# Two units instead of one by token halves ahead of norms 1 to 3 of a decoder trunk

## The chip, the cores and the metric

One core of one Trainium2 chip runs the whole kernel. The metric is the device time of one execution in microseconds. The trace comes from one profiled execution, times in it are microseconds from its start.

## The reference, cut to what matters

The input x is 512 tokens by 1024 channels in float32. Each of two layers does

```python
h = _modulate(_rmsnorm(x, norm_mix_g[l]), shift1, scale1)
x = x + gate1[:, None, :] * _mixer(h, ...)          # ends with: merged @ w_mix_out
h2 = _modulate(_rmsnorm(x, norm_mlp_g[l]), shift2, scale2)
u = jnp.square(jax.nn.relu(h2 @ w_up[l]))
x = x + gate2[:, None, :] * (u @ w_down[l])
```

and `_rmsnorm(x, final_g)` closes the trunk. A norm needs the mean of x*x over all 1024 channels of a token, so it can't begin for a token before the last channels of x have been added. The norms are numbered 0 (layer 0, mixer), 1 (layer 0, MLP), 2 (layer 1, mixer), 3 (layer 1, MLP) and 4 (final).

## The kernel before, in words

**Layout.** x is held transposed, `x_T`: 8 tiles k of 128 channels, 512 tokens wide. Every matrix product of 32-bit values is three matmuls of a shorter format: weights and activations are split into a high half (`w_hi`, `h_hi` or `y_hi`) and the rest (`w_lo`, `h_lo` or `y_lo`), and the products hi*hi, hi*lo and lo*hi are summed in PSUM.

**Units.** The work of TensorE is cut into units of 256 output channels, with two halves j of 128 channels. `half_unit` (line 940) does one half for all 512 tokens: 8 tiles k by 3 matmuls, 24 in all, into the bank `proj[:, j]`. A unit's weights pass four hands. SyncE issues the load into `w_raw` (line 330; it waits until the low halves of the unit two before are made). ScalarE copies `w_raw` to `w_hi` (`split_weights`, line 464; in one operation, or in two pieces). GpSimd makes `w_lo` (line 425, four operations for each half of a unit, always in the order of the units). TensorE waits on `lo_ready`. `w_hi` and `w_lo` have four slots, that is two units: the weights of unit u + 2 can be split only when TensorE has ended the products of the same half of unit u, which ScalarE's `products` waits for.

**Ahead of a norm.** The last four units ahead of norms 1 to 3 (the mixer's output, units MIX to MIX+3, or the last quarter of the MLP's down projection, MLP+4 to MLP+7) each add two tiles of x. For a whole tile VectorE adds the product (`add_to_x`, line 1405), ScalarE squares the new x (`square`, line 447) and VectorE sums the squares (`add_square`, line 1300). The first three units go so. The last goes by token halves in `tail_unit` (line 1052): t is a half of 256 tokens, and the order is t=0 j=0, t=0 j=1, t=1 j=0, t=1 j=1, 24 matmuls of 256 columns each. Its adds are at lines 1413 (t=0) and 1416 (t=1), its squares at 452, its sum at 1308.

**The norm.** In the middle of the part t=1 j=0, TensorE does `mean_square` for t=0 (lines 1019 and 1021, a product with `ones`). ScalarE's `root` makes 1/sqrt by a logarithm and an exponential (495, 496). Then come 16 steps g, 8 tiles for t=0 and 8 for t=1. Each has a scale on VectorE into PSUM (`scale_step`, line 1425, on two alternating banks, so it waits for the low step two before), the high half on ScalarE (`high_half`, line 550) and the low half on VectorE (`low_step`, line 1432). Between them lie VectorE's remaining adds, and on ScalarE the root for t=1 (after g=4) and, at g = 6 to 9, the four pieces of the split of the unit after the next one.

**The normed unit.** The first unit behind the norm (`normed_unit`, line 1074, its matmuls at 1088) takes h as it comes: for t=0 tile by tile, j=0 and j=1 in turn, and for t=1 four tiles so and then the last four of j=0 and of j=1. Before the first matmul of each j it waits for that half's `lo_ready`. After the first two tiles of t=0 stands `mean_square` for t=1. TensorE takes its instructions strictly in this order, and so do the other engines.

## Time and profile before

| | us |
|---|---|
| runs shown | 2303.15, 2302.43, 2303.00; median 2303.0 |
| the profiled execution's own time | 2302.98 |
| its span, first to last instruction | 2301.3 |
| TensorE busy | 2273.9 (99% of the span) |
| VectorE busy | 1089.3 (47%) |
| ScalarE busy | 908.0 (39%) |
| GpSimd busy | 1147.4 (50%) |
| granted TensorE clock, mean | 0.999 |

A row of a timeline has the start, the duration, the engine, the line, the operation and its tiles (out<-in), the count where equal neighbours are merged, and in brackets how long the engine had been idle before it and which instruction released it. PE is TensorE, DVE VectorE, ACT ScalarE, POOL GpSimd, SPq the issuing queue of SyncE. Matmuls are pipelined: the time from the start of one to the start of the next says what one costs, not its duration.

### The profile page before, as it was taken

The page shows a single profiled execution, that of the slowest core. Times are in us where ns is not written, and L with a number is a line of the kernel's source. Part 1 is how long each engine was busy: PE and PEld are TensorE (multiplying, and loading weights), DVE is VectorE, ACT ScalarE, POOL GpSimd, SP SyncE. Part 2 cuts the span into 40 slices and gives each one's busy share as a digit, 9 for nine tenths or more (in the row PEclk, how much of TensorE's full clock was granted, in tenths as well). Part 3 has the DMA queues.
Part 4 walks back from the last instruction along what each step waited for, and adds up shares of the span by engine and source line. Part 5 has one row for each costly group of instructions (what it writes and reads, how often), then busy time and mean ns, then how long its engine had stood idle before and what let it go on. Part 6 is the DMA issues. An engine that isn't in the chain of part 4 may idle for free.

```text
span 2301.3 us, 28143 instructions
## 1 busy us (share of the span) xinstructions
PE 2273.9 (99%) x11378; PEld 1885.8 (82%) x11378; DVE 1089.3 (47%) x1497; ACT 908.0 (39%) x1125; POOL 1147.4 (50%) x1489
## 2 busy tenths in 40 slices
PE   7999999999999999999999999999999999999999
PEld 4888888888888888888888888888888788888887
DVE  5776568546653341121276757441666524221223
ACT  4332233256675242332333323232666834332332
POOL 3454554534455554555545455455444444555543
PEclk9999999999999999999999999999999999999999
DMA  9444544322222323323334444222222223233231
GB/s 300 135 151 147 169 133 146 129 74 74 74 92 74 107 86 101 101 92 93 109 120 151 160 141 139 78 92 92 76 72 73 74 92 92 96 103 95 92 97 69
DMA packets 244161, 252.49 MB, mean 110 GB/s; under 512 B 4016, under 2 KB 241728, under 8 KB 244032
## 3 DMA queue, kind: packets, MB, share of 16 engines
q1 hardware_dynamic: 242352, 247.00, 33.2%
q10 hardware_dynamic: 1680, 3.70, 0.5%
q8 instruction: 90, 1.47, 0.3%
q14 instruction: 39, 0.32, 0.0%
HBM read 248.59 MB, written 2.10 MB: 109 GB/s over the span
## 4 chain that ended last, share of the span: by engine, by line
PE 95%; DVE 2%; SPq 1%; DMA 1%; ACT 1%; issue 0%; DVEq 0%; ACTq 0%
PE proj L953 66%; PE proj L975 6%; PE proj L1009 4%; PE proj L992 4%; PE att L992 4%; PE att L1137 3%; PE att L1187 2%; PE att L1197 1%; PE att L1175 1%; PE att L1120 1%; PE proj L1070 1%; DVE att L1425 1%; SPq L339 1%; DVE h_lo L1432 1%; PE att L1150 1%; DMA first_y<-in_w_ada 1%
## 5 line engine op out<-in xcount | busy, mean ns | idle before, releaser
L425 POOL TENSOR_TENSOR w_lo<-w_raw,w_hi 128x256 fp32r<-128x256 f32 x1472 | 1145.3, 811 | 1124.3 <-ACT w_hi L471 985.5
L953 PE MATMUL proj<-h_hi,w_hi 128*128 128x512 f32 x1440 | 567.4, 394 | 0.0
L953 PE MATMUL proj<-h_hi,w_lo 128*128 128x512 f32 x1440 | 561.2, 390 | 0.0
L953 PE MATMUL proj<-h_lo,w_hi 128*128 128x512 f32 x1440 | 560.6, 389 | 0.0
L471 ACT ACTIVATE w_hi<-w_raw 128x1024 fp32r<-128x1024 f32 (+1 forms) x342 | 353.2, 1039 | 454.0 <-PE proj L953 278.5
L953 PEld LDWEIGHTS proj<-h_hi,w_lo 128*128 128x128 f32 x1440 | 270.3, 188 | 57.5
L953 PEld LDWEIGHTS proj<-h_hi,w_hi 128*128 128x128 f32 x1440 | 270.5, 188 | 56.3 <-issue 1.6
L953 PEld LDWEIGHTS proj<-h_lo,w_hi 128*128 128x128 f32 x1440 | 270.6, 188 | 54.1
L953 PE MATMUL proj<-y_hi,w_hi 128*128 128x512 f32 x800 | 311.2, 389 | 0.0
L953 PE MATMUL proj<-y_lo,w_hi 128*128 128x512 f32 x800 | 311.2, 389 | 0.0
L953 PE MATMUL proj<-y_hi,w_lo 128*128 128x512 f32 x800 | 311.2, 389 | 0.0
L1405 DVE SCALAR_TENSOR_TENSOR x_T<-proj,mod,x_T 128x512 f32<-128x512 f32 x72 | 54.1, 751 | 290.0 <-PE proj L953 290.0
L1318 DVE SCALAR_TENSOR_TENSOR slab<-slab,c_act 128x256 f32<-128x256 f32 x280 | 176.9, 632 | 9.9
L953 PEld LDWEIGHTS proj<-y_lo,w_hi 128*128 128x128 f32 x800 | 150.2, 188 | 31.3
L953 PEld LDWEIGHTS proj<-y_hi,w_lo 128*128 128x128 f32 x800 | 150.2, 188 | 31.2
L953 PEld LDWEIGHTS proj<-y_hi,w_hi 128*128 128x128 f32 x800 | 150.2, 188 | 31.0
L1713 DVE TENSOR_TENSOR work<-work 128x512 f32<-128x512 f32 x64 | 45.7, 714 | 207.0 <-ACT work L804 207.0
L480 ACT ACTIVATE w_hi<-w_raw 128x512 fp32r<-128x512 f32 x64 | 37.0, 625 | 200.8 <-PE proj L992 130.9
L804 ACT ACTIVATE work<-proj 128x512 f32<-128x512 f32 x64 | 38.2, 597 | 159.4 <-PE proj L953 156.9
L1614 DVE TENSOR_TENSOR_SCAN slab<-slab,work 128x1280 f32<-128x1280 f32 x32 | 91.4, 2855 | 1.1
L1612 DVE SCALAR_TENSOR_TENSOR work<-att,work 128x1280 f32<-128x1280 f32 x32 | 47.6, 1487 | 61.0 <-ACT work L702 61.0
L1009 PE MATMUL proj<-w_hi,h_hi 128*128 128x256 f32 x256 | 73.1, 286 | 0.0
(252 smaller groups left out, 3202.8 us busy)
## 6 DMA issues: line engine op xcount, KB each, us to landing
w_raw<-in_w_in SPq DMA_DIRECT2D x88, 1024.0 KB, 5.1
slab<-in_w_ada SPq DMA_DIRECT2D x42, 1024.0 KB, 6.7
w_raw<-in_w_up SPq DMA_DIRECT2D x32, 1024.0 KB, 5.3
w_raw<-in_w_down SPq DMA_DIRECT2D x32, 1024.0 KB, 5.1
w_raw<-in_w_ret_out SPq DMA_DIRECT2D x16, 1024.0 KB, 5.4
w_raw<-in_w_sb_out SPq DMA_DIRECT2D x8, 1024.0 KB, 5.1
w_raw<-in_w_mix_out SPq DMA_DIRECT2D x8, 1024.0 KB, 5.1
first_y<-in_w_ada SPq DMA_DIRECT2D x4, 1024.0 KB, 12.4
```

Source lines behind the costliest of these rows:

```text
L425: ins = pool.tensor_tensor(w_lo[:, slot, k:k + 2, :], w_raw[:, s, k:k + 2, P * j:P * (j + 1)], w_hi[:, slot, k:k + 2, :], ALU.subtract)
L471: ins = act.activation(w_hi[:, 2 * s + j, ks, :], w_raw[:, s, ks, P * j:P * (j + 1)], ACT.Copy)
L953: last = pe.matmul(proj[:, j, :], w[:, slot, k, :], a[:, k, :], start=k == 0 and n == 0, stop=k == KT - 1 and n == 2)
L975: last = pe.matmul(proj[:, j, :], w[:, slot, k, :], a[:, k, :], start=k == 0 and n == 0, stop=k == KT - 1 and n == 2)
L992: last = pe.matmul(v_of(t).rearrange("p (a n) -> p a n", a=4), a[:, k, t * P:(t + 1) * P], w[:, :, k, :], start=k == 0 and n == 0, stop=k ...
L1009: last = pe.matmul(proj[:, t // 2, UNIT * (t % 2):UNIT * (t % 2 + 1)].rearrange("p (a n) -> p a n", a=2), a[:, k, t * P:(t + 1) * P], w[:, ...
L1137: last = pe.matmul(att[:, RET_BANKS[t], :], p[:, at:at + P], v[:, j, :], start=j == 0 and n == 0, stop=j == t and n == 2)
L1187: last = pe.transpose(att_flat[:, at:at + P], logits[:, a, row_at(i) + P * j:row_at(i) + P * (j + 1)], ident[:, :])
L1318: ins = dve.scalar_tensor_tensor(acc, raw[:, k, :], c_act[:, k:k + 1], acc, ALU.mult, ALU.add)
L1405: free(dve.scalar_tensor_tensor(x_T[:, k, :], proj[:, half, :], mod[:, ds(gate_col + k, 1)], x_T[:, k, :], ALU.mult, ALU.add), half)
L1612: own.link(dve.scalar_tensor_tensor(terms[:, a, :], scores_of(a), 0.0, terms[:, a, :], ALU.max, ALU.add))
L1614: own.link(dve.tensor_tensor_scan(logits[:, a, ::-1], carry_t[:, ::-1], terms[:, a, ::-1], 0.0, ALU.mult, ALU.add))
```

## The change

The last two units ahead of norms 1 to 3 go by token halves, together: `tail_units` does t=0 for both units (four parts of 24 matmuls of 256 columns), then t=1 for both. The first mean square stands in the middle of the first part of t=1. The second unit of the two writes to the two late banks in both halves; a semaphore `late_free` says that its t=0 values have been taken. Squares and sums of tiles 4 to 7 become operations of 256 columns each. On ScalarE the split of the normed unit's own weights (unit + 2) stands at g = 1 to 4 in pieces, and that of the unit behind it (unit + 3) at g = 9 to 12. The root for t=1 stands after the eight high halves of t=0. VectorE does its remaining adds and sums between the steps for t=0, and the last add behind the eighth low step. Counters of squares and sums are rebased (`SQUARED`, `SUMMED`). The tail ahead of the final norm keeps its order.

```diff
@@ -74,6 +74,9 @@
 HALVES = (slice(0, HALF), slice(HALF, SEQ))
 NORM_STEPS = 2 * KT
 BIG = 3.0e38
+
+SQUARED = (0, 10, 22, 34, 46)
+SUMMED = (0, 8, 18, 28, 38)
 
 RET_UNITS = 6
...
+            def square_part(n, k, t, buffers):
+
+                added_before = 3 * t + k - 2 if k >= 6 else k - 2
+                act.wait_ge(sq_used, SUMMED[n] + 1 + added_before)
+                act.activation(buffers[0][:, k % 2, HALVES[t]], x_T[:, k, HALVES[t]], ACT.Square).then_inc(squared, 1)
+
             def norm_tail(n, pair, unit, buffers):
 
-                tail_first(n, pair, unit, buffers)
-                for g in range(NORM_STEPS):
+                for j in range(2):
+                    added(pair, unit, j)
+                    square_part(n, 4 + j, 0, buffers)
+                for j in range(2):
+                    act.wait_ge(late_free, 2 * (n - 1) + j + 1)
+                    square_part(n, 6 + j, 0, buffers)
+                root(n, 0)
+                added(pair, unit + 1, 0)
+                square_part(n, 4, 1, buffers)
+                for g in range(KT):
                     high_half(n, g)
-                    if g == 3:
-                        tail_second(n, buffers)
-                    if g == 4:
-                        root(n, 1)
-                    if g in (6, 8):
-                        products(pair, unit, (g - 6) // 2)
-                    if 6 <= g < 10:
-                        split_weights(pair, unit + 2, (g - 6) // 2, g % 2)
+                    if g == 2:
+                        added(pair, unit + 1, 1)
+                        square_part(n, 5, 1, buffers)
+                    if g == 6:
+                        act.wait_ge(tail_added, 2 * n - 1)
+                        square_part(n, 6, 1, buffers)
+                    if g in (1, 3):
+                        products(pair, unit, g // 2)
+                    if g in (1, 2, 3, 4):
+                        split_weights(pair, unit + 2, (g - 1) // 2, (g - 1) % 2)
+                act.wait_ge(tail_added, 2 * n)
+                square_part(n, 7, 1, buffers)
+                root(n, 1)
+                for g in range(KT, NORM_STEPS):
+                    high_half(n, g)
+                    if g in (9, 11):
+                        products(pair, unit + 1, (g - 9) // 2)
+                    if 9 <= g < 13:
+                        split_weights(pair, unit + 3, (g - 9) // 2, (g - 9) % 2)
...
+            def tail_units(n, pair, unit, hi, lo, buffers):
+
+                for t in range(2):
+                    for m in range(2):
+                        for j in range(2):
+                            slot = 2 * ((unit + m) % 2) + j
+                            if t == 0:
+                                pe.wait_ge(lo_ready, 8 * pair + 4 * (unit + m) + 2 * (j + 1) + LO_CREDIT)
+                            if m == 0:
+                                pe.wait_ge(bank_free[j], 2 * pair + unit + 1 + t)
+                            elif t == 1:
+                                pe.wait_ge(late_free, 2 * (n - 1) + j + 1)
+                            dst = proj[:, j, HALVES[0]] if m == 0 else tail_late(j)
+                            for k in range(KT):
+                                if (t, m, j, k) == (1, 0, 0, KT // 2):
+                                    mean_square(n, 0, buffers)
+                                for i, (w, a) in enumerate(((w_hi, hi), (w_hi, lo), (w_lo, hi))):
+                                    last = pe.matmul(dst, w[:, slot, k, :], a[:, k, HALVES[t]],
+                                                     start=k == 0 and i == 0, stop=k == KT - 1 and i == 2)
+                            last.then_inc(tail_done if t == 0 else proj_done, 1)
...
-            def norm(n, between):
-
+            def add_part_square(n, k, t, buffers):
+
+                dve.wait_ge(squared, SQUARED[n] + 4 * t + k + 1)
+                dve.wait_ge(sq_used, SUMMED[n] + 3 * t + k)
+                sq_sum = buffers[1][:, HALVES[t]]
+                dve.tensor_tensor(sq_sum, sq_sum, buffers[0][:, k % 2, HALVES[t]], ALU.add).then_inc(sq_used, 1)
+
+            def add_part(n, k, t, pair, unit, gate_col):
+
+                m, j = (k - 4) // 2, k % 2
+                gate, x = mod[:, ds(gate_col + k, 1)], x_T[:, k, HALVES[t]]
+                if t == 0:
+                    dve.wait_ge(tail_done, 4 * (n - 1) + k - 3)
+                else:
+                    products(pair, unit + m, j)
+                ins = dve.scalar_tensor_tensor(x, proj[:, j, HALVES[0]] if m == 0 else tail_late(j), gate, x,
+                                               ALU.mult, ALU.add)
+                ins.then_inc(bank_free[j] if m == 0 else tail_added if t else late_free, 1)
+
+            def norm_tail(n, pair, unit, gate_col, buffers):
+
+                def part_of(k, t):
+                    add_part(n, k, t, pair, unit, gate_col)
+
+                add_square(n, 3, buffers)
+                part_of(4, 0)
+                part_of(5, 0)
+                add_part_square(n, 4, 0, buffers)
+                part_of(6, 0)
+                add_part_square(n, 5, 0, buffers)
+                part_of(7, 0)
+                add_part_square(n, 6, 0, buffers)
                 dve.wait_ge(mods_ready, n)
-                for g in range(NORM_STEPS + 1):
+                for g in range(KT):
+                    scale_step(n, g)
+                    if g == 0:
+                        part_of(4, 1)
+                    if g == 2:
+                        add_part_square(n, 4, 1, buffers)
+                    if g == 3:
+                        part_of(5, 1)
+                    if g >= 1:
+                        low_step(n, g - 1)
+                    if g == 4:
+                        add_part_square(n, 5, 1, buffers)
+                    if g == 6:
+                        part_of(6, 1)
+                    if g == 7:
+                        add_part_square(n, 6, 1, buffers)
+                low_step(n, KT - 1)
+                part_of(7, 1)
+                for g in range(KT, NORM_STEPS + 1):
                     if g < NORM_STEPS:
                         scale_step(n, g)
-                    if g in between:
-                        between[g]()
-                    if g >= 1:
+                    if g > KT:
                         low_step(n, g - 1)
-
-            def norm_tail(n, pair, unit, gate_col, buffers):
-
-                add_square(n, 5, buffers)
-                add_tail(n, 0, 0, pair, unit, gate_col)
-                add_last_square(n, 0, buffers)
-                add_tail(n, 1, 0, pair, unit, gate_col)
-                between = {0: lambda: add_tail(n, 0, 1, pair, unit, gate_col),
-                           2: lambda: add_last_square(n, 1, buffers),
-                           3: lambda: add_tail(n, 1, 1, pair, unit, gate_col)}
-                norm(n, between)
```

The loops ahead of the tails are one unit shorter on all engines: `range(2)` for `range(3)` ahead of norms 1 and 3, and two units for three in the last `down` of layer 0, with `norm_tail` and `tail_units` called on MIX + 2 and MLP + 6.

## Rows read from the trace of the kernel before

**Rows 1.** Timeline of TensorE around norm 1: start us, us, engine, line, operation.

```profile
785.79 0.39 PE L953 MATMUL proj<-h_hi,w_hi 128*128 128x512 f32 x1
...
796.67 0.28 PE L1070 MATMUL proj<-h_hi,w_hi 128*128 128x256 f32 x1
...
803.87 0.60 PE L1019 MATMUL att<-work,ones 128*128 128x256 f32 x2
...
804.85 0.28 PE L1070 MATMUL att<-h_lo,w_hi 128*128 128x256 f32 x1
...
809.04 0.28 PE L1088 MATMUL proj<-h_hi,w_hi 128*128 128x256 f32 x1
...
810.49 0.60 PE L1019 MATMUL att<-work,ones 128*128 128x256 f32 x2
...
822.49 0.39 PE L1088 MATMUL proj<-h_hi,w_hi 128*128 128x256 f32 x1
...
824.38 0.40 PE L953 MATMUL proj<-h_hi,w_hi 128*128 128x512 f32 x1
```

**Rows 2.** Waits of TensorE, whole run: us in total, times, longest us.

```profile
PE att L843 <- DMA decay_t<-in_final_g: 7.8, 1, 7.8
...
PE proj L1088 <- DVE h_lo L1432: 1.8, 6, 0.3
```

**Rows 3.** Timeline of VectorE around norm 1.

```profile
799.75 0.48 DVE L1413 SCALAR_TENSOR_TENSOR x_T<-proj,mod,x_T 128x256 f32<-128x256 f32 x1 [0.40 <-PE proj L1070]
...
800.72 0.90 DVE L1308 TENSOR_TENSOR work<-work 128x256 f32<-128x256 f32 x1 [0.49 <-ACT work L452]
...
805.88 0.49 DVE L1425 SCALAR_TENSOR_TENSOR att<-x_T,n_scale,att 128x256 f32<-128x256 f32 x1 [2.77 <-ACT att L496]
...
807.75 0.48 DVE L1432 SCALAR_TENSOR_TENSOR h_lo<-att,n_shift,h_hi 128x256 fp32r<-128x256 f32 x1 [0.51 <-ACT h_hi L550]
...
808.27 0.49 DVE L1425 SCALAR_TENSOR_TENSOR att<-x_T,n_scale,att 128x256 f32<-128x256 f32 x1
...
808.67 0.42 DVE L1308 TENSOR_TENSOR work<-work 128x256 f32<-128x256 f32 x1
...
814.54 0.49 DVE L1425 SCALAR_TENSOR_TENSOR att<-x_T,n_scale,att 128x256 f32<-128x256 f32 x1
...
821.95 0.48 DVE L1432 SCALAR_TENSOR_TENSOR h_lo<-att,n_shift,h_hi 128x256 fp32r<-128x256 f32 x1 [0.15 <-ACT h_hi L550]
```

**Rows 4.** Timeline of VectorE around norm 2.

```profile
1153.88 0.48 DVE L1413 SCALAR_TENSOR_TENSOR x_T<-proj,mod,x_T 128x256 f32<-128x256 f32 x1 [0.40 <-PE proj L1070]
...
1176.03 0.48 DVE L1432 SCALAR_TENSOR_TENSOR h_lo<-att,n_shift,h_hi 128x256 fp32r<-128x256 f32 x1 [0.15 <-ACT h_hi L550]
```

**Rows 5.** Timeline of ScalarE around norm 1.

```profile
800.26 0.42 ACT L452 ACTIVATE work<-x_T 128x256 f32<-128x256 f32 x1 [1.77 <-DVE x_T L1413]
...
806.88 0.42 ACT L452 ACTIVATE work<-x_T 128x256 f32<-128x256 f32 x1 [1.10 <-DVE x_T L1416]
...
807.24 0.84 ACT L550 ACTIVATE h_hi<-att,n_shift 128x256 fp32r<-128x256 f32 x2
...
814.46 0.62 ACT L471 ACTIVATE w_hi<-w_raw 128x512 fp32r<-128x512 f32 x1
...
832.40 1.04 ACT L471 ACTIVATE w_hi<-w_raw 128x1024 fp32r<-128x1024 f32 x1
```

**Rows 6.** Timeline of GpSimd around norm 1, operations merged (xcount).

```profile
798.05 3.28 POOL L425 TENSOR_TENSOR w_lo<-w_raw,w_hi 128x256 fp32r<-128x256 f32 x4 [2.17 <-ACT w_hi L471]
...
815.16 5.60 POOL L425 TENSOR_TENSOR w_lo<-w_raw,w_hi 128x256 fp32r<-128x256 f32 x8 [13.82 <-ACT w_hi L471]
```

**Rows 7.** Line 425 from 797.9 to 801.5 us: duration ns min/median/max.

```profile
L425 POOL TENSOR_TENSOR w_lo<-w_raw,w_hi x4: 737/741/1192, 798.1 to 800.6; 128x256 fp32r<-128x256 f32 x4
```

**Rows 8.** DMA issues of the page: KB each, us to landing.

```profile
w_raw<-in_w_up SPq DMA_DIRECT2D x32, 1024.0 KB, 5.3
```

**Rows 9.** First 20 us: busy us by engine, granted clock, DMA share, GB/s.

```profile
0.00:20.00 20.00, 8.16 (x50) 6.20 (x50) 7.62 (x17) 9.53 (x15) 2.10 (x17) 1.00 0.94 313
```

More of the change, by code:

```diff
@@ L788, in _ @@
                         split_weights(first, SB_OUT + m + 2, half)
-                for m in range(3):
+                for m in range(2):
                     for half in range(2):
@@ L794, in _ @@
                         square(2 * layer + 1, 2 * m + half, at_mlp)
-                norm_tail(2 * layer + 1, first, MIX + 3, at_mlp)
+                norm_tail(2 * layer + 1, first, MIX + 2, at_mlp)
                 if layer < DEPTH - 1:
@@ L810, in down @@
                 def down(pair, last):
-                    for m in range(3 if last else 4):
+                    for m in range(4 if not last else 2 if layer < DEPTH - 1 else 3):
                         for half in range(2):
                             products(pair, MLP + 4 + m, half)
-                            if not last or m < 2 or layer < DEPTH - 1:
+                            if not last or m < 2:
                                 split_weights(pair, MLP + 4 + m + 2, half)
@@ L1050, in turn_first_tokens, with final_unit @@
                             last.then_inc(y_turned, 1)
-            def tail_unit(n, pair, unit, hi, lo, buffers, final=False):
+            def final_unit(pair, unit, hi, lo, buffers):
                 for t in range(2):
                     for j in range(2):
-                        if final and t == j == 1:
+                        if t == j == 1:
                             turn_first_tokens(pair, unit)
@@ L1064, in tail_unit @@
                             if (t, j, k) == (1, 0, KT // 2):
[L1065 to L1068 removed]
+                                final_mean_square(0, buffers)
                             for m, (w, a) in enumerate(((w_hi, hi), (w_hi, lo), (w_lo, hi))):
@@ L1234, in _ @@
                 whole_unit(first, GB_LAST, h_hi, h_lo)
-                for m in range(7):
+                for m in range(6):
                     hi, lo, unit = (y_hi, y_lo, SB_OUT + m) if m < 4 else (h_hi, h_lo, SB_OUT + m)
@@ L1240, in _ @@
                         half_unit(first, unit, half, hi, lo, tile_ready if half == 0 else None)
-                tail_unit(2 * layer + 1, first, MIX + 3, h_hi, h_lo, at_mlp)
+                tail_units(2 * layer + 1, first, MIX + 2, h_hi, h_lo, at_mlp)
                 def quarter(pair, f):
@@ L1248, in quarter @@
                             whole_unit(pair, MLP + m, h_hi, h_lo)
-                    for m in range(4 if f < QUARTERS - 1 else 3):
+                    for m in range(4 if f < QUARTERS - 1 else 2 if layer < DEPTH - 1 else 3):
                         for half in range(2):
@@ L1257, in _ @@
                 quarter(first + 4 * (QUARTERS - 1), QUARTERS - 1)
-                tail_unit(2 * layer + 2, first + 4 * (QUARTERS - 1), MLP + 7, y_hi, y_lo, at_layer,
-                          layer == DEPTH - 1)
+                if layer < DEPTH - 1:
+                    tail_units(2 * layer + 2, first + 4 * (QUARTERS - 1), MLP + 6, y_hi, y_lo, at_layer)
+                else:
+                    final_unit(first + 4 * (QUARTERS - 1), MLP + 7, y_hi, y_lo, at_layer)
             n = 2 * DEPTH
@@ L1295, in add_square @@
                 if 1 <= k <= KT - 2:
-                    dve.wait_ge(squared, 10 * n + (k + 1 if k < 6 else 8))
+                    dve.wait_ge(squared, SQUARED[n] + (k + 1 if k < 6 else 8))
                     if k >= 2:
-                        dve.wait_ge(sq_used, 8 * n + k)
+                        dve.wait_ge(sq_used, SUMMED[n] + k)
                     sq, sq_sum = buffers[0], buffers[1]
@@ L1687, in _ @@
                 gates = MODS * KT * layer
-                for m in range(7):
+                for m in range(6):
                     for half in range(2):
@@ L1702, in _ @@
                             add_to_x(first, SB_OUT + m, half, k, gates + KT * GATE1)
-                norm_tail(2 * layer + 1, first, MIX + 3, gates + KT * GATE1, at_mlp)
+                norm_tail(2 * layer + 1, first, MIX + 2, gates + KT * GATE1, at_mlp)
                 def quarter(pair, f, last):
@@ L1717, in quarter @@
                                               ALU.subtract).then_inc(u_split, 1)
-                    for m in range(3 if last else 4):
+                    for m in range(4 if not last else 2 if layer < DEPTH - 1 else 3):
                         for half in range(2):
```

30 lines of the change are left out of this document (14 added, 16 removed).

## The prediction, made before the changed kernel ran

> **What bounds the kernel now.** I read the page first (TensorE busy in 99% of the span), then TensorE's waits, then the timelines around one norm, engine by engine. TensorE is the bound nearly everywhere, so only two things about a norm can move the time: how much TensorE is given to do there, and where it is held up. All times t below count from the start of the last unit but one ahead of norm 1, at 785.79 us [rows 1].
>
> The reader is to see four marks on TensorE [rows 1]: the last unit begins at t=10.88 (48 matmuls of 512 columns behind, 0.227 us each); the normed unit begins at 23.25; its mean square comes 1.45 us into it; and the next unit begins at 38.59. A matmul of 256 columns costs 0.120 us from start to start (35 of them between 804.85 and 809.04), and a mean square in the middle adds 0.86 us (803.87 to 804.85 less one matmul). The 192 matmuls of 256 columns between t=10.88 and 38.59 are worth 23.0 us, the two mean squares 1.8. So 27.71 - 24.8 = 2.9 us are lost in small gaps before matmuls of the normed unit. The list of waits names only 1.8 us for all norms together, six waits of 0.3 us at most [rows 2]; the rest is too short to be listed but is there in the sum.
>
> These gaps come from VectorE's chain. The scale of step 8 starts at t=28.75 and the low half of step 15 at 36.16 [rows 3]: 7.41 us for eight steps, 0.91 to 0.93 each, while TensorE needs 0.72 for a tile (six matmuls). The last low half sets the end: the tile's first matmul starts 0.54 us behind it (822.49), then 15 matmuls remain, and 824.38 is reached. The second norm has the same distance from its first late add to its last low half, 22.15 us against 22.20 [rows 3, 4], and the six waits are two for each of three norms. I take the three as equal, and their losses as 8.7 us together: the most that the change could give back.
>
> **The change, part by part.** *Matmuls.* One more unit goes in 96 matmuls of 256 columns in place of 48 of 512: 11.50 us for 10.88, so +0.62 us for each norm, on TensorE itself, with nothing to hide it. The normed unit can start at t=23.87 at the earliest.
>
> *The first root.* The mean square for t=0 now stands at 4.5 parts, t=12.94. Its sum waits for the add of tile 7, t=0, which can start at 11.71: the part ends at 11.50, and the first late add started 0.20 us behind its part (796.67 plus 24 matmuls is 799.55; 799.75 in [rows 3]). Its square starts 0.51 us later [rows 3, 5] and ends at 12.64, in time. From the mean square to the first scale took 2.01 us [rows 1, 3]. So the first scale is at 14.95 where it was at 20.09, and the first eight steps have nine microseconds ahead of the normed unit. The gaps of its first half go.
>
> *The order on VectorE and ScalarE.* I follow it with these lags, all from rows: 0.49 from a dependent scale or add to the next on VectorE, 0.40 if independent (808.27 to 808.67), 0.51 to ScalarE's operation on it, 0.36 from a square to the next operation, 0.51 from a high half to its low half, 0.52 from that to the next scale on its bank [rows 3, 5]. Scale 0 at 14.95, add of tile 4 (t=1) 15.44, its square 15.95, high half 0 16.31, low half 0 16.8, scale 2 17.3, low half 1 18.1, scale 3 18.6, add of tile 5 19.0, its square 19.5. Only then comes the second piece of the split of the normed unit's weights, half j=0, at 19.87; the pieces for j=1 follow behind high halves 3 and 4, the last at 21.7. Before, these weights had been split in whole operations during the last plain unit, and their low halves were made by 801.33 (t=15.5) [rows 6]; nobody waited.
>
> *The low halves.* A piece takes 0.62 us and GpSimd starts 0.08 behind its end (814.46 and 815.16) [rows 5, 6]. So GpSimd starts on half j=0 at 20.56. Four operations take 2.80 us when nothing disturbs them (5.60 for eight) and 3.28 when one is stretched from 0.74 to 1.19 us [rows 6, 7]. Half j=0 is ready at 23.4 to 23.8, just as TensorE comes to it. Half j=1 is ready at 26.2 to 27.1, and TensorE needs it at 24.2, behind the first three matmuls. It stands for 2.0 to 2.9 us. This wait is new. Behind it on TensorE are all further matmuls, and among them the mean square for t=1, so ScalarE's root, VectorE's scale 8 and everything of the second half wait for it as well.
>
> *The second half.* After the wait come nine matmuls (1.08 us) and the mean square at 27.3 to 28.2. The add of tile 7 (t=1), late in VectorE's list, is at 25.5 to 26.3 and its square by 27.2, so that cover holds. Then +2.01 to scale 8 at 29.4 to 30.3, against 28.75 before, +7.2 to 7.4 to the last low half (the pieces of the next unit's split stand between its high halves, as four did in the first half before), +0.54 and 1.80 for 15 matmuls: the end is at 38.9 to 39.9, where it was 38.59. TensorE has kept pace by then: from the mean square, 0.86 and 87 matmuls give 38.6 to 39.5, less than the chain by 0.3.
>
> *Which value.* The low halves decide. VectorE's sum of squares with both inputs in SBUF (line 1308) took 0.90 us beside GpSimd and 0.42 alone [rows 3], and one of GpSimd's four operations was stretched by 0.45 in the stretch where two such sums (one of 512, one of 256 columns) ran [rows 6, 7]. The new order puts two 256-column sums, of tiles 5 and 6, into the 5.7 us of GpSimd's work. Between no stretch and a full one for each, I take half: +0.4 on the lower end, the nearest row being one in which a smaller sum cost VectorE rather than GpSimd. With 0.1 for the split pieces in the chain, the end is at about 39.3 to 39.4: +0.7 us a norm.
>
> The Trainium skill (SBUF — State Buffer, section "Who interferes with whom") says that a VectorE instruction with two SBUF inputs and a GpSimd instruction that reads SBUF lock each other out, the later one standing until the first ends. By that rule both sides pay at each meeting, and the sum would go to its upper end, +1.2 us a norm. The two durations of line 1308 agree with it.
>
> *What else moves, at nothing.* The 256-column adds, squares and sums of tiles 4 and 5 replace whole ones and lie beside TensorE's parts with 1 us or more to spare; if that cover went, the mean square for t=0 would be late by the excess. The loads: the unit behind the normed one had its low halves by t=35.0 [rows 6], now by 38.2 to 40, so SyncE issues the load two units on about 4 us later. It lands 5.3 us on [rows 8], at 43.5 to 45.3, and ScalarE splits it at 46.6 [rows 5] plus the shift of the end. The cover left is about 2 us. In norm 2 the loads behind it on SyncE's queue (the ada rows) move with it.
>
> **The sum.** 3 x (+0.7) = +2.1 us. The profiled execution took 2302.98, the median is 2303.0, so the sum stands against either: 2305. The bounds are 3 x 0.3 and 3 x 1.3: 2303.9 to 2306.9. About 0.2% (4.6 us) is what a measurement of this kernel can tell from no change.
>
> **The rivals.** *A: the split comes early enough.* If TensorE hardly waits for j=1 (the pieces earlier, or GpSimd faster than in any row), the add of tile 7 and its square set the mean square at about 26.1, scale 8 comes at 28.1 and the end at 37.6: -1.0 us a norm, 2300. If VectorE's chain kept pace too, only TensorE's own 0.62 and one mean square would be left: 36.3, -2.3 a norm, 2296, the only way to a measurable gain. For it: 9 us of room for the first eight steps. Against it: the square of tile 5 stands ahead of the split on ScalarE, and 2 x 2.8 us of GpSimd's work can't fit into the 3.6 us from 20.56 to 24.2.
>
> *B: the pause costs TensorE its clock.* The place is the new wait at the second half of the weights, 2 to 3 us in one piece, where today no wait around a norm is over 0.3. If the granted clock fell there from 2.4 to 1.2 GHz for the rest of the normed unit, its 93 matmuls would take 0.12 us more each: +11 us for a norm, and slower than 2303 by over 4.6 from a single such norm: 2316 for one, 2338 for three. Against it: in the first 20 us of the run TensorE is busy for 8.2 us only, with a first wait of 7.8 us, and its granted clock is 1.00 [rows 2, 9]. The Trainium skill (TensorE: Matmul & The Clock Gate, "Why this matters for your kernels") warns that idle gaps between bursts of matmuls bring the clock back to half; the trace here shows gaps as long without a fall.
>
> *C: GpSimd or the loads slip further.* If every one of the eight low operations were as stretched as the worst (1.19 us), they would end 3 us later than the upper end, +4 us a norm, 2315. It takes more than the two sums in 5.7 us; one stretched operation in four is all that rows show.
>
> **How the numbers follow.** The forecast (the wait for the low halves, +0.3 to +1.3 a norm) has 0.80. A without a measurable gain has 0.08, with one 0.03. B has 0.04, C and a load that lands too late 0.05. Faster by over 0.2%: 0.03. Within: 0.88. Slower: 0.09. The range is the forecast's 2303.9 to 2306.9, with 2 us below for lags that I have too long, towards A, and 0.6 above for a short slip of a load: 2301.8 to 2307.5.
>
> **What would show it.** In the changed profile: 0.62 us more of TensorE's matmuls a norm; the first scale 14.95 us behind the first tail unit's start; TensorE's longest wait at line 1088's successor, for GpSimd's line 425, three times, 2.0 to 2.9 us; scale 8 at 29.4 to 30.3; the normed unit's end at 38.9 to 39.9. No such wait, or a wait for ScalarE's square in its place, would be rival A; a granted clock under 1.00 in the normed unit, rival B; low operations of more than 3.3 us for four, rival C. The forecast falls if the time is under 2301 or over 2308.

## The result, and the profile after

| kernel | runs | lowest | median | highest (us) |
|---|---|---|---|---|
| before | 20 | 2302.43 | 2303.33 | 2304.33 |
| changed | 20 | 2304.79 | 2306.53 | 2308.37 |

One run of the kernel before took 3187.36 us, 880 us more than any other, and is left out of the highest value. The ratio is 1.0014 (95% interval 1.0008 to 1.002): the changed kernel is 3.2 us slower, within 0.2% and within the range. Its runs lie further apart, 3.6 us from lowest to highest against 1.9. The profiled execution took 2307.48 us.

The page's first lines, of the changed kernel:

```profile
span 2305.7 us, 28461 instructions
...
PE 2275.1 (99%) x11522; PEld 1894.5 (82%) x11522; DVE 1092.9 (47%) x1509; ACT 909.9 (39%) x1137; POOL 1145.3 (50%) x1489
```

TensorE is busy for 1.2 us more than before, the span is 4.4 us longer. The other 3.2 us are time in which TensorE stood. A stretch at a slower clock counts as busy. Of TensorE's waits (engine, line, releaser: us in total, times, longest), the second is new and answers to [rows 2]:

```profile
PE att L871 <- DMA decay_t<-in_final_g: 7.5, 1, 7.5
...
PE proj L1134 <- POOL w_lo L428: 6.2, 3, 2.1
```

Three waits for GpSimd's low halves, 6.2 us together, 2.1 at most, in place of six of 0.3 us for VectorE. The clearest look at them is norm 3, where the clock stays up. TensorE from the start of the two tail units (answers to [rows 1]):

```profile
1917.91 0.28 PE L1068 MATMUL proj<-h_hi,w_hi 128*128 128x256 f32 x1
...
1941.80 0.28 PE L1134 MATMUL proj<-h_hi,w_hi 128*128 128x256 f32 x1
...
1944.38 0.39 PE L1134 MATMUL proj<-h_hi,w_hi 128*128 128x256 f32 x1 [2.06 <-POOL w_lo L428]
...
1957.08 0.40 PE L981 MATMUL proj<-h_hi,w_hi 128*128 128x512 f32 x1
```

GpSimd there, eight low operations of the normed unit's weights:

```profile
1938.40 5.93 POOL L428 TENSOR_TENSOR w_lo<-w_raw,w_hi 128x256 fp32r<-128x256 f32 x8 [15.82 <-ACT w_hi L474]
```

VectorE there (the sums of squares of tiles 5 and 6 at line 1488, scale 8 at 1947.51, the last low half):

```profile
1939.11 0.99 DVE L1488 TENSOR_TENSOR work<-work 128x256 f32<-128x256 f32 x1
...
1942.90 0.85 DVE L1488 TENSOR_TENSOR work<-work 128x256 f32<-128x256 f32 x1
...
1947.51 0.88 DVE L1473 SCALAR_TENSOR_TENSOR att<-x_T,n_scale,att 128x256 f32<-128x256 f32 x2 [2.98 <-ACT att L499]
...
1954.65 0.48 DVE L1480 SCALAR_TENSOR_TENSOR h_lo<-att,n_shift,h_hi 128x256 fp32r<-128x256 f32 x1 [0.15 <-ACT h_hi L553]
```

Counted from 1917.91: the normed unit starts at 23.89, GpSimd starts at 20.49 and ends at 26.42, TensorE goes on at 26.5, scale 8 is at 29.60, the last low half at 36.74, the end at 39.17. In the kernel before the end was at 38.59, 38.81 and 38.53 around norms 1, 2 and 3. The two sums of squares beside GpSimd took 0.99 and 0.85 us where one alone takes 0.42 [rows 3].

Norm 1 of the same trace looks the same up to the wait, and then differs. TensorE by windows (window, length, busy us, granted clock, DMA share, GB/s):

```profile
808.00:812.00 4.00, 3.33 (x28) 1.00 0.01 4
...
812.00:814.00 2.00, 0.61 (x4) 0.94 0.00 0
...
814.00:817.00 3.00, 3.00 (x12) 0.50 0.77 224
...
817.00:820.00 3.00, 3.00 (x26) 0.97 0.35 125
...
1167.00:1170.00 3.00, 0.93 (x8) 1.00 0.01 3
...
1170.00:1173.00 3.00, 3.00 (x24) 1.00 0.78 246
```

The reader is to see three things: in the two windows from 808 to 814 TensorE stands idle for over 2 us; from 814 to 817 its granted clock is 0.50, that is 1.2 GHz; and in norm 2 (1167 to 1173) the same pause is followed by a clock of 1.00. In the slow stretch the matmuls of 256 columns come 0.21 to 0.22 us apart instead of 0.12:

```profile
810.81 0.28 PE L1134 MATMUL proj<-h_hi,w_hi 128*128 128x256 f32 x1
...
814.53 0.41 PE L1134 MATMUL proj<-h_hi,w_hi 128*128 128x256 f32 x1
...
814.75 0.41 PE L1134 MATMUL proj<-h_lo,w_hi 128*128 128x256 f32 x1
...
827.57 0.40 PE L981 MATMUL proj<-h_hi,w_hi 128*128 128x512 f32 x1
```

The normed unit of norm 1 takes 16.76 us (810.81 to 827.57), that of norm 3 15.27 (1941.81 to 1957.08). A fall of the clock costs 1.5 us here. Against the kernel before, the end comes 2.07 us later around norm 1 (40.66), and 0.64 later around norm 2 (39.45) and norm 3 (39.17). The stretches from one norm's end to the next tail's start are the same in both traces within 0.02 us.

There is one more, in a stage that the change doesn't touch. From 20 to 27 us, changed and before:

```profile
20.00:27.00 7.00, 6.34 (x28) 0.76 1.10 348
```

```profile
20.00:27.00 7.00, 4.77 (x28) 1.00 1.10 348
```

The same 28 matmuls, at a mean clock of 0.76 and of 1.00. The first tail unit starts at 786.91 instead of 785.79, 1.1 us later in this execution. So the 4.5 us between the two profiled executions are 1.9 for the normed units' later ends (3 x 0.64), 1.4 more for the fall at norm 1 and 1.1 ahead of all norms, in code that the change leaves as it was. That all of this 1.1 is the early fall's is not shown. In the five traces without an early fall the first tail unit (the last unit but one) starts at 785.79 to 786.39; in those with one it starts at 786.91, 787.03 and 787.09 (changed, e6, e1), but also at 785.96 and 786.15 (e7, e4), where the fall cost nothing visible.

### The profile page after: what moved, and what is told of

Same layout as the page of the kernel before. It is cut to its first block, busy times and chain, and to the rows that moved or that the text cites. A ratio compares the mean times of both kernels' runs of the same rounds, so it can differ in the third digit from the quotient of the medians.

```text
span 2305.7 us, 28461 instructions
## 1 busy us (share of the span) xinstructions
PE 2275.1 (99%) x11522; PEld 1894.5 (82%) x11522; DVE 1092.9 (47%) x1509; ACT 909.9 (39%) x1137; POOL 1145.3 (50%) x1489
## 4 chain that ended last, share of the span: by engine, by line
PE 95%; DVE 2%; ACT 1%; POOL 1%; issue 1%; DMA 0%; DVEq 0%; SPq 0%; ACTq 0%
PE proj L981 65%; PE proj L1003 6%; PE proj L1037 4%; PE proj L1020 4%; PE att L1020 4%; PE att L1183 3%; PE att L1233 2%; PE att L1243 1%; PE att L1221 1%; PE att L1166 1%; PE proj L1068 1%; PE proj L1134 1%; POOL w_lo L428 1%; PE att L1068 1%; PE att L1196 1%
## 5 line engine op out<-in xcount | busy, mean ns | idle before, releaser
L981 PE MATMUL proj<-h_hi,w_hi 128*128 128x512 f32 x1408 | 554.9, 394 | 0.0
L981 PE MATMUL proj<-h_hi,w_lo 128*128 128x512 f32 x1408 | 548.7, 390 | 0.0
L981 PE MATMUL proj<-h_lo,w_hi 128*128 128x512 f32 x1408 | 548.1, 389 | 0.0
L981 PEld LDWEIGHTS proj<-h_hi,w_lo 128*128 128x128 f32 x1408 | 264.2, 188 | 56.2
L981 PEld LDWEIGHTS proj<-h_hi,w_hi 128*128 128x128 f32 x1408 | 264.4, 188 | 55.4 <-issue 1.6
L981 PEld LDWEIGHTS proj<-h_lo,w_hi 128*128 128x128 f32 x1408 | 264.6, 188 | 52.5
L981 PE MATMUL proj<-y_hi,w_hi 128*128 128x512 f32 x784 | 305.0, 389 | 0.0
L981 PE MATMUL proj<-y_lo,w_hi 128*128 128x512 f32 x784 | 305.0, 389 | 0.0
L981 PE MATMUL proj<-y_hi,w_lo 128*128 128x512 f32 x784 | 305.0, 389 | 0.0
L981 PEld LDWEIGHTS proj<-y_lo,w_hi 128*128 128x128 f32 x784 | 147.1, 188 | 30.3
```

Source lines behind the costliest of these rows:

```text
L981: last = pe.matmul(proj[:, j, :], w[:, slot, k, :], a[:, k, :], start=k == 0 and n == 0, stop=k == KT - 1 and n == 2)
```

## The experiments

Two theories stand, and add: **the wait theory** (the low halves of the normed unit's weights hold TensorE, +0.6 us a norm) and **the clock theory** (the pause that this makes throws TensorE's clock in some executions, 1.5 us each time, and this spreads the runs and makes the rest of the difference). The rival to both: the extra narrow matmuls and something unseen.

All were timed in five rounds with the kernel before on the same chip, 11 runs each, e5 5 runs. The intervals of e1 and e6 include 1: by the runs alone these two can't be told from the kernel before.

| kernel | lowest | median | highest | ratio to before (95%) |
|---|---|---|---|---|
| e1 split early | 2301.29 | 2301.54 | 2302.30 | 0.9993 (0.9984 to 1.0001) |
| e2 pause filled | 2304.83 | 2305.73 | 2306.53 | 1.001 (1.0001 to 1.0019) |
| e3 narrow only | 2304.59 | 2305.06 | 2306.06 | 1.0009 (1.0 to 1.0018) |
| e4 order tuned | 2297.70 | 2298.12 | 2299.23 | 0.9978 (0.9969 to 0.9987) |
| before beside e1 to e4 | 2302.70 | 2303.22 | 2304.53 | |
| e5 split late | 2310.64 | 2312.47 | 2312.67 | 1.0039 (1.0025 to 1.0052) |
| r1 changed again | 2304.97 | 2306.23 | 2308.62 | 1.0012 (1.0004 to 1.0021) |
| before beside e5 and r1 | 2302.56 | 2303.17 | 2303.87 | |
| e6 vector order only | 2303.13 | 2303.72 | 2304.79 | 1.0003 (0.9994 to 1.0012) |
| e7 order tuned again | 2297.57 | 2297.93 | 2298.76 | 0.9978 (0.9969 to 0.9987) |
| before beside e6 and e7 | 2302.51 | 2303.10 | 2304.37 | |

### The narrow matmuls alone

```diff
@@ half_unit, of before.py @@
-                for k in range(KT):
+                for cols in HALVES if narrow else (slice(0, SEQ),):
+                    for k in range(KT):
...
-                        last = pe.matmul(proj[:, j, :], w[:, slot, k, :], a[:, k, :],
+                            last = pe.matmul(proj[:, j, cols], w[:, slot, k, :], a[:, k, cols],
```

`narrow` is set for the last unit but one ahead of norms 1 to 3.

> The kernel before, with the last unit but one ahead of norms 1 to 3 in matmuls of 256 columns by token halves, its order on all other engines as before. Theory: this term alone, 0.62 us a norm, 1.9 us: 2305.2 with before at 2303.3, no wait of TensorE over 0.3 us. Rival (the narrow matmuls are hidden in gaps of VectorE's chain): the chain starts later by the same time, so nothing hides; if they were hidden, 2303.3.

Measured 2305.06, 1.84 us over before beside it, where 1.86 (3 x 0.62) was worked out. The waits at the normed unit stay what they were:

```profile
PE proj L1089 <- DVE h_lo L1434: 1.8, 6, 0.3
```

So the price of the first part of the change stands whole on TensorE's path. The lowest run, 2304.59, is also within 0.2 us of the changed kernel's lowest, 2304.79, and in the traces the unit behind norm 3 ends at 39.19 here and at 39.17 in the changed kernel: what the earlier root gave back, the wait for the low halves took.

### The split of the weights earlier

```diff
@@ ScalarE's norm_tail, of the changed kernel @@
                 root(n, 0)
+                products(pair, unit, 0)
+                split_weights(pair, unit + 2, 0)
                 added(pair, unit + 1, 0)
...
-                    if g in (1, 3):
-                        products(pair, unit, g // 2)
-                    if g in (1, 2, 3, 4):
-                        split_weights(pair, unit + 2, (g - 1) // 2, (g - 1) % 2)
+                    if g == 1:
+                        products(pair, unit, 1)
+                        split_weights(pair, unit + 2, 1)
```

> Only ScalarE's split of the normed unit's weights is moved: half j=0 whole right behind the first root, half j=1 whole behind high half 1. Wait theory (the low halves hold TensorE): GpSimd starts 3.9 us earlier, the wait for it at the second half of the weights is gone, but a wait of 1.5 us in front of the second mean square takes its place, because the split delays the steps and the square of tile 7 by 0.5 us; the normed unit ends 38.3 us behind the first tail unit's start, against 38.6 before and 39.2 in the changed kernel without a clock fall: 2302.2. Clock theory (a pause of 2.3 us in one piece throws the clock now and then): with 1.5 us at most the falls around the norms get rare and the runs stand as close together as those of before. Rival (the extra matmuls and something else, not the weights, hold the time): no change against the changed kernel, 2304.8 or more.

2301.54, 1.7 us under before and 5.0 under the changed kernel, where 2302.2 was expected: only ScalarE's copies moved. GpSimd starts 3.8 us earlier, at 16.6 behind the start of the tail units (787.09):

```profile
803.73 5.99 POOL L428 TENSOR_TENSOR w_lo<-w_raw,w_hi 128x256 fp32r<-128x256 f32 x8 [11.97 <-ACT w_hi L474]
```

and TensorE takes the normed unit's first twelve matmuls without a wait, then stands at the second mean square:

```profile
787.09 0.28 PE L1069 MATMUL proj<-h_hi,w_hi 128*128 128x256 f32 x1
...
810.98 0.28 PE L1135 MATMUL proj<-h_hi,w_hi 128*128 128x256 f32 x1
...
812.42 0.65 PE L1048 MATMUL att<-work,ones 128*128 128x256 f32 x2
...
813.61 0.70 PE L1050 MATMUL att<-work,ones 128*128 128x256 f32 x2 [0.54 <-ACT work L574]
...
824.81 0.40 PE L982 MATMUL proj<-h_hi,w_hi 128*128 128x512 f32 x1
```

The mean square's second matmul starts 1.19 us behind its first, where 0.43 is usual; ScalarE's square of tile 7 (line 574) releases it. The wait there is 0.8 us, half of the 1.5 expected. The unit ends at 37.72 behind the start, 0.6 earlier than expected and 0.9 earlier than before; the three norms together make 2.5 us, but the medians show 1.7. The profiled execution of e1 has the fall in the window from 20 to 27 us and starts its first tail unit 1.3 us later than before. From norm 3's normed unit to the end of its span it takes 349.3 us where before (1952.60 to 2301.3) and the changed kernel (1957.08 to 2305.7) take 348.7; the 0.6 us lie behind the last matmul. How many of its other executions have either is not known, so 0.8 us stay open. The rival (nothing gained against the changed kernel) is out. Its runs span 1.0 us, the changed kernel's 3.6: without the long pause the spread goes, as the clock theory has it.

### The split of the weights later

```diff
@@ ScalarE's norm_tail, of the changed kernel @@
-                    if g in (1, 3):
-                        products(pair, unit, g // 2)
-                    if g in (1, 2, 3, 4):
-                        split_weights(pair, unit + 2, (g - 1) // 2, (g - 1) % 2)
+                    if g in (3, 5):
+                        products(pair, unit, (g - 2) // 2)
+                    if g in (3, 4, 5, 6):
+                        split_weights(pair, unit + 2, (g - 3) // 2, (g - 3) % 2)
```

> The changed kernel with the four pieces of the split two steps later (g = 3 to 6 instead of 1 to 4). Wait theory: GpSimd starts 1.3 us later, TensorE waits 1.0 us for half j=0 and 2.7 us for half j=1 of the normed unit's weights, and the unit ends 1.3 us later in each norm than in the changed kernel without a clock fall: its fastest runs are at 2304.8 + 3.9 = 2308.7. Clock theory: the pauses are longer (3.7 us with 0.4 us of work between them), so falls get more frequent, up to one in each norm at about 1.5 us: the median lies 2 to 5 us above the fastest runs. Rival (the weights are not what holds TensorE): no change against the changed kernel.

2312.47, and the lowest of five 2310.64, where the fastest were expected at 2308.7. Both weights' halves are waited for now, six times (us in total, times, longest):

```profile
PE proj L1134 <- POOL w_lo L428: 8.5, 6, 2.3
```

The profiled execution is the lowest one, and the clock fell in two of its three normed units (norms 1, 2 and 3 in turn):

```profile
813.00:816.00 3.00, 2.47 (x10) 0.50 0.38 84
...
1171.00:1174.00 3.00, 3.00 (x14) 0.57 0.76 241
...
1948.00:1951.00 3.00, 3.00 (x24) 1.00 0.71 204
```

Norm 3 has no fall and shows what the later split costs by itself:

```profile
1920.04 0.28 PE L1068 MATMUL proj<-h_hi,w_hi 128*128 128x256 f32 x1
...
1960.24 0.40 PE L981 MATMUL proj<-h_hi,w_hi 128*128 128x512 f32 x1
```

The end is at 40.20, 1.0 us later than in the changed kernel (39.17), where 1.3 was expected: 3.1 us for three norms. The two falls cost 1.3 and 1.2 us here (normed units of 16.93 and 17.05 us against 15.60 at norm 3, and 0.3 more at norm 2 in any kernel). 2310.64 less both is 2308.1, and the changed kernel's lowest run and 3.1 make 2307.9: the two agree. So the wait theory holds, a later split is a later end. That falls get more frequent rests on less: all five runs lie 2.7 us or more above 2307.9, which would be two falls or more in each. The longest single pause, 2.3 us, is hardly longer than the changed kernel's 2.1; another of 0.55 us stands ahead of it, with three matmuls between them.

### The pause filled

```diff
@@ normed_unit, of the changed kernel @@
+                            if t == k0 == 0 and j == 1:
+                                for _ in range(17):
+                                    pe.matmul(att[:, 1, HALF:SEQ], w_hi[:, slot - 1, 0, :], h_hi[:, 0, HALVES[0]],
+                                              start=True, stop=True)
                             if t == k0 == 0:
                                 pe.wait_ge(lo_ready, 8 * pair + 4 * unit + 2 * (j + 1) + LO_CREDIT)
```

> 17 idle matmuls of 256 columns (2.0 us) stand between the first three matmuls of the normed unit and the wait for the second half of its weights, into a part of PSUM that nobody reads. They lie inside the wait. Clock theory: TensorE is no longer idle, so its clock does not fall there, the granted clock is 1.00 in all three normed units, the runs gather near the lowest of the changed kernel, 2304.8, with the spread of before, 1.7 us lower than its median 2306.5. Rival (the spread of the changed kernel comes from loads or from elsewhere): median 2306.5 and the same spread as the changed kernel. If the idle matmuls stick out of the wait, 0.1 us a norm more.

The idle matmuls (line 1129) fill the wait to 0.19 us:

```profile
810.19 2.20 PE L1129 MATMUL att<-h_hi,w_hi 128*128 128x256 f32 x17
...
812.58 0.39 PE L1138 MATMUL proj<-h_hi,w_hi 128*128 128x256 f32 x1 [0.19 <-POOL w_lo L428]
```

and the granted clock around the three pauses is 1.00:

```profile
809.80:813.00 3.20, 3.01 (x25) 1.00 0.00 0
...
1164.70:1168.00 3.30, 3.23 (x27) 1.00 0.01 2
...
1939.40:1942.70 3.30, 3.23 (x27) 1.00 0.00 0
```

The lowest run is 2304.83, as the changed kernel's 2304.79: the filling costs nothing and gives nothing to the end of the chain. What goes is the upper part: 2306.53 is the highest of 11 runs, while 12 of the 31 runs of the changed kernel (10 of 20 and 2 of 11) lie above 2306.6, up to 2308.62. The spread, 1.7 us, is like before's 1.9. But the runs don't gather at the lowest as expected; they fill 1.7 us, and the median falls by 0.5 to 0.8 us, not 1.7. That was misjudged: before's own runs spread over 1.9 us, and I had counted all of the changed kernel's spread as falls at norms. Whether before's spread comes from falls in that early window is not shown; its one trace has none.

### The changed kernel once more

> The changed kernel once more, on the chip of the later split and with a new trace. Clock theory: the fastest runs again near 2304.8, about half of the runs 1.5 us or more above them, and the new trace shows falls at other norms or none (whether a pause of 2.1 us meets one is chance), each costing about 1.5 us; the normed units without one last 15.3 us. Rival (the fall at norm 1 belongs to that place): the same single fall at norm 1 again.

Lowest 2304.97, median 2306.23, 5 of 11 runs within 0.3 us of the lowest and the rest 1.2 us or more above. The new trace, norms 1, 2 and 3:

```profile
812.00:815.00 3.00, 2.30 (x10) 0.62 0.32 72
...
1171.00:1174.00 3.00, 3.00 (x26) 1.00 0.84 293
...
1945.00:1948.00 3.00, 3.00 (x24) 1.00 0.96 288
```

Again one fall, again at norm 1, and this time none in that early window. Here the rival can't be put aside by this run; the later split shows a fall at norm 2 as well, so the place is not bound to norm 1. But norm 1 fell in all three traces with such a pause, norm 2 in one and norm 3 in none, so a part of the rival stands. How often each norm is hit stays open.

### The order tuned

With the weights early, the square of tile 7 holds TensorE. VectorE's adds and sums for the second half can go ahead of first-half steps, since TensorE needs the last of these only by t=29.

```diff
@@ VectorE's norm_tail, of the changed kernel @@
-                for g in range(KT):
-                    scale_step(n, g)
...
+                steps = (("s", 0), ("x", 4), ("s", 1), ("q", 4), ("l", 0), ("s", 2), ("l", 1), ("x", 5), ("s", 3),
+                         ("l", 2), ("q", 5), ("s", 4), ("l", 3), ("x", 6), ("s", 5), ("l", 4), ("q", 6), ("s", 6),
+                         ("l", 5), ("x", 7), ("s", 7), ("l", 6), ("l", 7))
@@ ScalarE's norm_tail @@
+                    if g == 0:
+                        products(pair, unit, 0)
+                        split_weights(pair, unit + 2, 0, 0)
                     high_half(n, g)
+                    if g == 0:
+                        split_weights(pair, unit + 2, 0, 1)
...
```

Here s is a scale, l a low step, x an add and q a sum of squares. ScalarE has the pieces for j=1 and the squares of tiles 5 to 7 behind high halves 2, 3 and 5.

> The changed kernel with another order: the split of the normed unit's weights in pieces from high half 0 on, and VectorE's adds and sums for tiles 5 to 7, second token half, ahead of scales 3 to 7 instead of behind them. Wait theory: no wait for GpSimd, the second mean square is held up by 0.2 us only, scale 8 comes at 27.5 us behind the first tail unit's start (28.75 before), the normed unit ends at 37.0 against 38.6 before: 1.6 us a norm less than before, 2298.6. No fall of the clock. Rival (the tail is bound by VectorE's chain of steps whatever the order): the chain keeps 0.91 us a step, and if the first half's steps are in the way, the end is at 38 or more and the time 2301.5 or more.

2298.12, ratio 0.9978: it beats both kernels, before by 5.1 us and the changed one by 8.4. TensorE in norm 1:

```profile
786.15 0.28 PE L1073 MATMUL proj<-h_hi,w_hi 128*128 128x256 f32 x1
...
810.04 0.28 PE L1139 MATMUL proj<-h_hi,w_hi 128*128 128x256 f32 x1
...
811.49 0.60 PE L1052 MATMUL att<-work,ones 128*128 128x256 f32 x2
...
811.92 0.59 PE L1054 MATMUL att<-work,ones 128*128 128x256 f32 x2
...
823.02 0.40 PE L986 MATMUL proj<-h_hi,w_hi 128*128 128x512 f32 x1
```

No wait between 810.04 and 811.49, none between the two matmuls of the mean square (0.43 us). GpSimd had started at 17.9 behind 786.15 and was done at 24.05:

```profile
804.02 6.18 POOL L428 TENSOR_TENSOR w_lo<-w_raw,w_hi 128x256 fp32r<-128x256 f32 x8 [13.20 <-ACT w_hi L474]
```

VectorE: the sum of tile 6 ahead of the second mean square, scale 8 at 27.28 and the last low half at 34.43:

```profile
809.10 0.51 DVE L1493 TENSOR_TENSOR work<-work 128x256 f32<-128x256 f32 x1
...
813.43 0.88 DVE L1478 SCALAR_TENSOR_TENSOR att<-x_T,n_scale,att 128x256 f32<-128x256 f32 x2 [0.93 <-ACT att L499]
...
820.58 0.48 DVE L1485 SCALAR_TENSOR_TENSOR h_lo<-att,n_shift,h_hi 128x256 fp32r<-128x256 f32 x1 [0.15 <-ACT h_hi L553]
```

The end is at 36.87, 1.7 us earlier than before, and 3 x 1.7 is the 5.1 us measured. The rival, with its end at 38 or more, is out. What is left over TensorE's own 36.3 is VectorE's chain of 0.91 us a step.

> The tuned order once more, on the chip of the run with VectorE's order alone: 2298.1 again, all runs within 1.9 us as before has them, 5 us under the kernel before. Rival (the first result was of that chip): more than 1 us off.

2297.93 on another occasion, 5.2 us under the kernel before beside it: the gain holds.

### VectorE's order alone

The tuned kernel with the four pieces of the split back behind high halves 1 to 4:

```diff
@@ ScalarE's norm_tail, of the tuned kernel @@
-                    if g == 0:
-                        products(pair, unit, 0)
-                        split_weights(pair, unit + 2, 0, 0)
                     high_half(n, g)
-                    if g == 0:
-                        split_weights(pair, unit + 2, 0, 1)
+                    if g == 1:
+                        products(pair, unit, 0)
+                    if g in (1, 2):
+                        split_weights(pair, unit + 2, 0, g - 1)
...
```

> The tuned order's half: VectorE's and ScalarE's adds, squares and sums for tiles 5 to 7 as in the tuned order, but the four pieces of the split behind high halves 1 to 4 as in the changed kernel. Wait theory (two limits in series, the low halves and then the square of tile 7): the wait for GpSimd stays, 1.9 us, and the normed unit ends at 38.7 behind the first tail unit's start, 0.4 us earlier than in the changed kernel and 1.7 later than in the tuned order: fastest runs at 2303.6, some runs 1.5 us higher for a fall of the clock. Rival (VectorE's order alone gives the gain): 2298.5 as the tuned order.

2303.72, where 2303.6 was expected. The wait for GpSimd stays:

```profile
PE proj L1139 <- POOL w_lo L428: 5.0, 3, 1.7
```

The unit ends at 38.78 (787.03 to 825.81), where 38.7 was expected. So an earlier split alone (e1's, in whole operations) gives 5.0 us against the changed kernel's median and VectorE's order alone 2.8 (fewer falls of the clock among them), both together 8.4. Without falls, an end that was at 39.2 comes at 37.7, 38.8 and 36.9: 1.5, 0.4 and 2.3 us, and the two together give more than their sum. They are two limits behind each other: TensorE first stands for the low halves, and once these are early, for the square of tile 7.

## Why the prediction was right, and where it was off

**The bound and the matmuls.** +0.62 us a norm on TensorE's path: shown, 1.84 us for three by the narrow matmuls alone.

**The first root and the order behind it.** Scale 0 was worked out at 14.95 and came at 14.97 (801.88 in the changed trace of norm 1, from 786.91); GpSimd's start at 20.56, and came at 20.49. The lags read from rows of before carried through some fifteen steps on two engines.

**The low halves.** This step decided, as forecast: the new wait is there three times, 2.1 us listed against 2.0 to 2.9, and the kernels with the split earlier and later move the end with it. Their duration was taken as 6.1 us (5.7 and 0.4 for disturbance) and measured 5.93. The rule that the Trainium skill gives (SBUF — State Buffer, "Who interferes with whom"), that the later of two such instructions stands until the first ends, the trace bears out in kind. At each of the two meetings VectorE's sum was stretched, to 0.99 and 0.85 us from the 0.42 that it takes alone, and so was the GpSimd operation that began during the sum, to 0.92 and 0.90 us where the median is 0.74. But GpSimd paid less than the one stretched operation of before had made me expect: 0.3 us for both together (5.93 against 5.60 [rows 6]), where the sum has 0.4 and its upper end 0.9. So the upper end wasn't reached.

**The second half.** Scale 8 at 29.60 (29.4 to 30.3 was worked out), the end at 39.17 (38.9 to 39.9, 39.3 to 39.4 taken): +0.6 a norm where +0.7 stood. One count in it was wrong without changing the result: behind the mean square stand 84 matmuls, not 87, so that TensorE's own work left it 0.7 us ahead of the chain, not 0.3. The loads and the other moved steps cost nothing visible: from norm 1's end to the next tail's start it is 315.54 us before and 315.55 after, from norm 2's end to the third tail's start 735.34 in both.

**The sum.** +2.1 was forecast and +3.2 measured. Without falls of the clock the trace gives 3 x 0.64 = 1.9, and the narrow kernel, which has the same end of the normed unit, agrees with 1.84. The other 1.3 us come from something that the sum held at nothing. That the median still lies in the range is owed to the range's width: in that part it is luck. Filling the pause took 0.5 to 0.8 us off the median. That part is rival B, which I had as an alternative with a chance of 0.04; it is an addition, and comes in a part of the runs. The remaining 0.5 to 0.8 us are not assigned: they are less than the spread of either kernel. Two things were wrong in rival B. Its price was 11 us, with the low clock taken to last for the rest of the normed unit; in the trace it lasts from 814 to 817 us and costs 1.5. And its chance: I held against it that the first 20 us show a wait of 7.8 us at a granted clock of 1.00 [rows 2, 9]. That was a misreading. The matmuls right behind that wait, in the same trace of before, run at half pace, 0.21 us apart, and from 13.7 us on the same matmuls are 0.11 us apart:

```profile
11.57 1.06 PE L854 MATMUL att<-ident,ya 128*128 128x128 f32 x4
...
14.35 0.82 PE L854 MATMUL att<-ident,ya 128*128 128x128 f32 x6
```

The window from 10 to 13.6 us is listed with a clock of 1.00 all the same, so this figure can't be trusted there, and the long wait was no evidence against B. (Whether the clock fell in that wait or hadn't risen yet can't be told: no matmul stands ahead of it.) One gap of that trace does speak against B: from 15.4 to 17.7 us TensorE stood for 2.3 us, and the clock stayed at 1.00. From 30 us on the kernel before has no pause of TensorE over 0.9 us, so its trace had nothing to price B with. What the Trainium skill says (TensorE: Matmul & The Clock Gate, "Why this matters for your kernels"), that idle gaps between bursts bring the clock back to half, the traces of the changed kernel and of the later split agree with, for pauses of 2.1 to 2.3 us in one piece; filled pauses showed no fall. Three traces with such pauses have a fall in four of nine norms; the trace of e6, with pauses of 1.7 us, has none in three. More is not known of how often.

**Rivals A and C.** A was right about what comes next: with the weights early, the end was at 37.7 against the 37.6 worked out. But as built the wait for the weights stood in front of it. Nothing of C was seen: eight low operations took 5.9 us in the changed kernel, and 6.2 at most in the others (e4).

**What the change did with its gain.** The gaps of 2.9 us a norm that the earlier root was to close are closed: behind the wait the normed unit runs without one until its last tiles. The time came back in one piece of 2.1 us ahead of them, because the weights of that unit, once ready almost 8 us early (15.5 against 23.25), had become the last thing to arrive.

## What to carry to other kernels

When a stage is widened so that a chain starts earlier, list everything else that the next stage needs and that was tied to the end of the old stage: here the buffers of the next weights came free only at t=15.2, and their way over two engines ended at 26.4. Work the new order out for every engine, with lags from rows; then look which item is last, move it, and do the same again: with the first limit gone, the next one still cost 0.8 us a norm (e1 against e4). Here many short gaps on TensorE were cheaper than one long one: 2.9 us a norm in gaps of 0.3 at most had no fall, a pause of 2.1 us cost the clock on top in some executions. And a clock of 1.00 in the first microseconds of a profile should be checked against the distance between equal matmuls.

## What the runs showed that I had not expected

- The granted clock fell to 0.50 (1.2 GHz) behind pauses of 2.1 to 2.3 us in some executions and not in others, in the middle of a run in which TensorE is busy for 99%. Each fall cost 1.2 to 1.6 us (16.76 against 15.27 us for the normed unit in the changed kernel).
- The kernel before has a spread of 1.9 us of its own; what makes it is not shown. The mean clock from 20 to 27 us is 0.76 in the traces of the changed kernel, e1, e4, e6 and e7, and 1.00 in those of before, e2, e3, e5 and r1, though all do the same there. The starts of the first tail unit, ahead of which all these kernels run the same code, differ by up to 1.3 us between the ten profiled executions, which is more than half of what three norms lost. Single profiled executions are best compared stretch by stretch.
